# Seven block products of a feed-forward pair, woven between ordinary slots

## The chip, the cores and the metric

The kernel runs on one core of one Trainium2 chip. The metric is the device time of one execution in microseconds; the kernel before takes 2487.53 us, the median of three runs (2485.97 to 2489.61). The engines are TensorE (PE in the profile, its weight loads PEld), VectorE (DVE), ScalarE (ACT), GpSimd (POOL) and SyncE (SP), which issues nearly all DMAs from one queue, in order.

## The reference

Two transformer-like layers run on 256 positions of width 2048, in float32. The part that the change touches is the feed-forward of the second layer:

```
h2 = rmsnorm(x, g_ffn)                      # 256 x 2048
gu = h2 @ w_gu                              # 2048 x 11264: gate half and up half
x  = x + (silu(gu[..., :5632]) * gu[..., 5632:]) @ w_down
```

The output has to agree with this float32 reference.

## The kernel before

**Tiles.** Positions are two tiles of 128 (`TT`), an output chunk is 512 columns (`W`), and a weight slot is 256 rows by 512 columns (`KS` = 2 blocks of 128 rows, 512 KB). To keep float32 accuracy every weight slot is split in two: ACT rounds it (`w_hi`, L1282), DVE takes the remainder (`w_lo`, L1945), and PE makes three matmuls in the place of one (activation high by weight low, high by high, low by high). An ordinary slot is 12 matmuls: 2 row blocks, 2 position tiles, 3 parts. `raw`, `w_hi` and `w_lo` are rings of 4 buffers. So slot g can be rounded when PE is done with slot g-4 (semaphore `slot_used`), its remainder follows, and PE waits for `lo_ready`. A raw buffer is free for the next load when the remainder is taken.

**Blocks and pairs.** The feed-forward runs in three blocks (`ff_block`) of 4, 4 and 3 pairs, each followed by a down projection. A pair makes one chunk of 512 gate columns (unit 0, `acc[:, 0]`) and the same chunk of up columns (unit 1, `acc[:, 1]`), over 8 slots of weight rows for each.

**Quad products.** In all pairs but the first, ten in number, the first two weight-row slots of gate and up (a two by two arrangement of weight blocks against a two by two arrangement of activation blocks) are not multiplied as eight block products but as seven, by sums of blocks (a Strassen-Winograd scheme). A product slot is 6 matmuls. The four weight blocks of a pair land in `quad_raw` (`load_quad`, L469; block 0 and 1 are gate and up of the first rows, 2 and 3 of the second), four in-place additions on DVE (`quad_add`, L1928, semaphore `quad_sum`) form the sums between the remainders that need them, and each sum is again rounded and split. The other 12 slots of a pair are ordinary (`after_quad`, L827 to L829).

**Order in a pair.** The seven products are slots 0 to 6, in the accumulators `tp[0]`, `acc[0,0]`, `po`, `sc`, `tp[1]`, `acc[0,1]`, `acc[1,0]`; slots 7 to 12 are gate and 13 to 18 up. ACT and DVE each walk a list written out by hand: roundings or remainders of the slots, and between them the rest. For ACT that is a copy of `tp[0]` (L1324), the silu of the gate chunk (L1334), the joining of transposed planes (L917) and their rounding (L928). For DVE it is the sum that ends the previous pair's up chunk (`up_out`, L2027), the gated product (L2018), its split in two 16-bit planes (L1406), three combining additions (L2060, L2064, L2068), the gate chunk (L2078) and the remainder of the joined planes (`lo_of`, L1414).

**SP's queue.** `load_ff` loads raw slot r when raw slot r-4 has had its remainder taken. The next pair's four blocks follow the loads 4 to 7 of a pair. The previous pair's planes are transposed by two DMAs (`turn_planes`, L366) ahead of load 6. A wait holds everything behind it on the queue.

Of the kernel before, what the change touches and what calls it, by code (L numbers as in the profile page):

```python
# [67 lines left out]
def feed_forward_slots():  # L68
# [46 lines left out]
def build_program(nc, t):  # L115
    ctx = ExitStack()
    with ctx:
# [232 lines left out]
        def _(sp):  # L350
# [121 lines left out]
            for b in range(3):  # L472
                for j in range(FF_PAIRS[b]):
# [3 lines left out]
                    for i in range(2 * n):  # L477
# [3 lines left out]
                        if j and i == n:  # L481
                            turn_planes(X_FF + b * NCH + j - 1, "ff")
                        load_ff(r + i, gate_up(b, j, unit, s))
                        if j < FF_PAIRS[b] - 1 and 4 <= i < 8:
                            load_quad(p + 1, i - 4)
                _, r = FF_DOWN[b]
                n = FF_SLOTS[b]
                for i in range(NCH * n):
# [4 lines left out]
                    if b < 2 and 20 <= i < 24:  # L493
                        load_quad(4 * b + 4, i - 20)
# [13 lines left out]
        def _(pe):  # L508
# [274 lines left out]
            def quad_product(g, f, out, xh, xl, start, stop=False):  # L783

                pe.wait_ge(lo_ready, g + f + 1)
                ring = (g + f) % RING
                for k in range(KS):
                    wh, wl = w_hi[:, ring, k, :], w_lo[:, ring, k, :]
# [9 lines left out]
            def quad_slots(p, u):  # L798
# [17 lines left out]
            def after_quad(g0, unit):  # L816

                for s in range(Q0, SPU):
                    g = g0 + s - Q0
                    pe.wait_ge(lo_ready, g + 1)  # L820
                    for k in range(KS):
                        for tk in range(TT):
                            kt, out = KS * s + k, acc[:, unit, tk, :]
                            xh, xl = (part[:, kt, tk * P:(tk + 1) * P] for part in (a_hi, a_lo))
                            wh, wl = w_hi[:, g % RING, k, :], w_lo[:, g % RING, k, :]
                            first = (unit, tk, s, k) == (1, 1, Q0, 0)
                            nc.tensor.matmul(out, xh, wl, start=first, stop=False)  # L827
                            nc.tensor.matmul(out, xh, wh, start=False, stop=False)  # L828
                            mm = nc.tensor.matmul(out, xl, wh, start=False,  # L829
                                                  stop=s == SPU - 1 and k == KS - 1)  # L830
                    mm.then_inc(slot_used, 1)

            def ff_block(b):
# [3 lines left out]
                for j in range(pairs):  # L837
                    p = pair_of(b, j)
                    g, _, quad = FF_PAIR[p]
                    if quad:  # L840
                        quad_slots(p, u + 2 * j)
                        after_quad(g + QUAD, 0)
                        after_quad(g + QUAD + SPU - Q0, 1)
# [1403 lines left out]
```

## Time and profile before

| what | value |
|---|---|
| median of three runs | 2487.53 us |
| profiled execution | 2487.44 us, span 2485.6 us, granted clock 0.999 |
| PE busy | 2466.3 us (99%) |
| DVE busy | 1608.4 us (65%) |
| ACT busy | 1409.5 us (57%) |
| DMA queue of SP | 66.1% of 16 engines' time |
| chain that ended last | PE 89%, DVE 6%, DMA 2%, ACT 2% |

The span is the time from the first to the last instruction of the execution that was profiled, and 1.84 us lie around it. Matmuls overlap, so that PE counts as busy nearly always; what it loses is read from its idle time and from the distance between starts of matmuls. The pairs lie between 1806 and 2404 us of the span, with the down projections between them.

### The profile page before, as it was taken

What the parts mean: (1) busy time and instruction counts of PE and PEld (TensorE: products, weight loads), DVE (VectorE), ACT (ScalarE), POOL (GpSimd) and SP (SyncE); (2) the same over time, 40 slices, a digit from 0 to 9 for tenths busy, and PEclk for the clock granted to TensorE, in tenths of its full rate; (3) what the DMA queues carried; (4) which work ended last, traced back from release to release, by engine and by line L of the source; (5) the groups of instructions that cost most, each with busy time, mean ns of one, the idle gap of its engine ahead of it and who ended that gap; (6) DMA issues with size and microseconds to landing.
All of it is one profiled execution on the core that took longest, in us unless ns stands there. A gap on an engine that the chain in (4) does not pass through costs nothing.

```text
span 2485.6 us, 28783 instructions
## 1 busy us (share of the span) xinstructions
PE 2466.3 (99%) x10957; PEld 2038.9 (82%) x10957; DVE 1608.4 (65%) x1743; ACT 1409.5 (57%) x1716; POOL 67.0 (3%) x78
## 2 busy tenths in 40 slices
PE   9999999999999999999999999999999999999999
PEld 8888888888888888888888888888787888788887
DVE  5988576556555565666577645556587567866774
ACT  6886566455455465556666644546555445554453
POOL 0110000000000000011100000000000000000000
PEclk9999999999999999999999999999999999999999
DMA  8997668677677676577766666667757765575755
GB/s 287 262 268 205 203 191 223 208 215 226 195 210 209 192 218 196 161 222 213 218 185 206 193 196 202 203 187 221 223 167 212 232 198 185 172 222 183 237 176 169
DMA packets 348554, 515.34 MB, mean 207 GB/s; under 512 B 113840, under 2 KB 114152, under 8 KB 348168
## 3 DMA queue, kind: packets, MB, share of 16 engines
q1 hardware_dynamic: 343592, 496.63, 66.1%
q0 software_dynamic: 4688, 16.93, 3.0%
q8 instruction: 86, 1.41, 0.2%
q14 instruction: 44, 0.36, 0.0%
q10 hardware_dynamic: 144, 0.01, 0.0%
HBM read 476.52 MB, written 4.47 MB: 194 GB/s over the span
## 4 chain that ended last, share of the span: by engine, by line
PE 89%; DVE 6%; DMA 2%; ACT 2%; issue 1%; SPq 1%; POOL 0%; DVEq 0%; ACTq 0%; POOLq 0%
PE acc L531 26%; PE acc L533 26%; PE acc L532 26%; DVE w_lo L1945 3%; PE acc L829 3%; PE acc L828 3%; PE acc L827 3%; DMA raw<-w_gu_dram 1%; DVE quad_raw L1928 1%; ACT w_hi L1282 1%; DMA planesT_mix<-planes_mix 0%; ACT joined_ff L917 0%; SPq L366 0%; DVE ev L2027 0%; PE tp L567 0%
## 5 line engine op out<-in xcount | busy, mean ns | idle before, releaser
L1371 DVE TENSOR_TENSOR w_lo<-raw,w_hi 128x1024 fp32r<-128x1024 f32 x628 | 761.2, 1224 | 539.6 <-ACT w_hi L880 539.0
L880 ACT ACTIVATE w_hi<-raw 128x1024 fp32r<-128x1024 f32 x628 | 659.3, 1059 | 639.1 <-PE acc L533 628.4
L531 PE MATMUL acc<-w_lo,a_hi 128*128 128x512 f32 x1664 | 652.2, 392 | 4.0 <-DVE a_lo L1420 3.2
L533 PE MATMUL acc<-w_hi,a_lo 128*128 128x512 f32 x1664 | 648.7, 390 | 0.0
L532 PE MATMUL acc<-w_hi,a_hi 128*128 128x512 f32 x1664 | 648.5, 390 | 0.0
L531 PE MATMUL acc<-w_lo,b_hi 128*128 128x512 f32 x1104 | 430.0, 389 | 0.3 <-DVE w_lo L1371 0.3
L532 PE MATMUL acc<-w_hi,b_hi 128*128 128x512 f32 x1104 | 429.5, 389 | 0.0
L533 PE MATMUL acc<-w_hi,b_lo 128*128 128x512 f32 x1104 | 429.5, 389 | 0.0
L1945 DVE TENSOR_TENSOR w_lo<-raw,w_hi 128x1024 fp32r<-128x1024 f32 x220 | 267.3, 1223 | 184.2 <-ACT w_hi L1282 183.3
L1282 ACT ACTIVATE w_hi<-raw 128x1024 fp32r<-128x1024 f32 x220 | 232.0, 1059 | 250.4 <-PE acc L533 111.8
L531 PEld LDWEIGHTS acc<-w_lo,a_hi 128*128 128x128 f32 x1664 | 313.1, 188 | 69.4 <-DVE a_lo L1420 3.7
L533 PEld LDWEIGHTS acc<-w_hi,a_lo 128*128 128x128 f32 x1664 | 313.0, 188 | 65.9
L532 PEld LDWEIGHTS acc<-w_hi,a_hi 128*128 128x128 f32 x1664 | 313.2, 188 | 64.2
L531 PEld LDWEIGHTS acc<-w_lo,b_hi 128*128 128x128 f32 x1104 | 207.2, 188 | 43.5 <-DVE w_lo L1371 0.7
L533 PEld LDWEIGHTS acc<-w_hi,b_lo 128*128 128x128 f32 x1104 | 207.2, 188 | 43.1
L532 PEld LDWEIGHTS acc<-w_hi,b_hi 128*128 128x128 f32 x1104 | 207.2, 188 | 43.0
L827 PE MATMUL acc<-w_lo,a_hi 128*128 128x512 f32 x480 | 186.7, 389 | 0.0
L828 PE MATMUL acc<-w_hi,a_hi 128*128 128x512 f32 x480 | 186.7, 389 | 0.0
L829 PE MATMUL acc<-w_hi,a_lo 128*128 128x512 f32 x480 | 186.7, 389 | 0.0
L1282 ACT ACTIVATE w_hi<-quad_raw 128x1024 fp32r<-128x1024 f32 x70 | 72.7, 1058 | 70.1 <-DVE quad_raw L1928 34.2
L828 PEld LDWEIGHTS acc<-w_hi,a_hi 128*128 128x128 f32 x480 | 90.1, 188 | 18.7
L827 PEld LDWEIGHTS acc<-w_lo,a_hi 128*128 128x128 f32 x480 | 90.1, 188 | 18.7
(259 smaller groups left out, 1900.8 us busy)
## 6 DMA issues: line engine op xcount, KB each, us to landing
raw<-w_in_dram SPq DMA_DIRECT2D x272, 512.0 KB, 4.5
raw<-w_down_dram SPq DMA_DIRECT2D x216, 512.0 KB, 4.2
raw<-w_gu_dram SPq DMA_DIRECT2D x136, 512.0 KB, 4.6
raw<-w_up_dram SPq DMA_DIRECT2D x128, 512.0 KB, 3.8
raw<-w_out_dram SPq DMA_DIRECT2D x64, 512.0 KB, 4.2
quad_raw<-w_gu_dram SPq DMA_DIRECT2D x40, 512.0 KB, 5.8
raw<-w_branch_dram SPq DMA_DIRECT2D x32, 512.0 KB, 4.2
tap_sum<-tap_add POOLq DMA_DIRECT2D x20, 512.0 KB, 7.1
```

Of the source, the lines that this page charges most:

```text
L531: nc.tensor.matmul(out, xh, wl, start=s == 0 and k == 0, stop=False)
L532: nc.tensor.matmul(out, xh, wh, start=False, stop=False)
L533: mm = nc.tensor.matmul(out, xl, wh, start=False, stop=s == n - 1 and k == KS - 1)
L827: nc.tensor.matmul(out, xh, wl, start=first, stop=False)
L828: nc.tensor.matmul(out, xh, wh, start=False, stop=False)
L829: mm = nc.tensor.matmul(out, xl, wh, start=False, stop=s == SPU - 1 and k == KS - 1)
L880: nc.scalar.activation(w_hi[:, ring], raw[:, ring], ACT.Copy).then_inc(hi_ready, 1)
L1282: nc.scalar.activation(w_hi[:, g % RING], src, ACT.Copy).then_inc(hi_ready, 1)
L1371: nc.vector.tensor_tensor(w_lo[:, ring], raw[:, ring], w_hi[:, ring].bitcast(F32), ALU.subtract).then_inc(lo_ready, 1)
L1928: nc.vector.tensor_tensor(quad_raw[:, to // 2, to % 2], quad_raw[:, one // 2, one % 2], quad_raw[:, other // 2, other % 2], ALU.add).then_ ...
L1945: nc.vector.tensor_tensor(w_lo[:, g % RING], src, w_hi[:, g % RING].bitcast(F32), ALU.subtract).then_inc(lo_ready, 1)
```

## The change

The seven products become slots 0, 2, 4, 6, 8, 10 and 12 of the pair, and the six ordinary gate slots lie between them as slots 1, 3, 5, 7, 9 and 11. The order of the products is new (accumulators `tp[0]`, `po`, `sc`, `acc[1,0]`, `tp[1]`, `acc[0,0]`, `acc[0,1]`). The up slots stay 13 to 18. The four additions stand after the remainders of slots 0, 1, 5 and 9. The next pair's blocks are loaded in the order 1, 3, 2, 0 after the loads 6, 7, 9 and 10 of a pair (after loads 17, 20, 23 and 26 of a down projection), each with waits of its own. The transposes move ahead of load 10. On DVE and ACT the combining additions, the planes' split, the silu and the joining stand at later places, among the up slots. No matmul, rounding, remainder, addition or load is added or taken away.

The diff, cut to its core ("..." marks what is left out):

```diff
@@ feed_forward_slots
             if quad:
-                kind += [(f, None) for f in range(QUAD)]
+                for f in range(QUAD):
+                    kind += [(f, None)] + [(None, r + f)] * (f < SPU - Q0)
             n = 2 * (SPU - Q0 if quad else SPU)
-            kind += [(None, r + i) for i in range(n)]
+            kind += [(None, r + i) for i in range(n // 2 if quad else 0, n)]
@@ sync: load_quad
-                if i == 0:
-                    if quad_of(p):
-                        sp.wait_ge(lo_ready, FF_PAIR[p - 1][0] + QUAD)
-                    else:
-                        sp.wait_ge(slot_used, G_FF)
+                if quad_of(p) == 0:
+                    sp.wait_ge(slot_used, G_FF)
+                else:
+                    g, q = FF_PAIR[p - 1][0], quad_of(p) - 1
+                    sp.wait_ge(lo_ready, g + (13, 5, 11, 7)[i])
+                    sp.wait_ge(quad_sum, 4 * q + (4, 2, 4, 3)[i])
...
-                        if j and i == n:
+                        if j and i == (10 if quad else n):
                             turn_planes(X_FF + b * NCH + j - 1, "ff")
                         load_ff(r + i, gate_up(b, j, unit, s))
-                        if j < FF_PAIRS[b] - 1 and 4 <= i < 8:
-                            load_quad(p + 1, i - 4)
+                        if j < FF_PAIRS[b] - 1 and (i if quad else i - 4) in (6, 7, 9, 10):
+                            load_quad(p + 1, {6: 1, 7: 3, 9: 2, 10: 0}[i if quad else i - 4])
@@ tensor: quad_pair (before: quad_slots and two after_quad)
-                quad_product(g, 0, tp[:, 0, :], *tile_of(0, 0), True, True)
+                quad_product(g, tp[:, 0, :], tile_of(0, 0))
                 pe.wait_ge(evacuated, u - 1)
-                quad_product(g, 1, acc[:, 0, 0, :], *tile_of(1, 0), True)
-                quad_product(g, 2, po[:, :], x_hi[:, 0], x_lo[:, 0], True, True)
-                quad_product(g, 3, sc[:, :], x_hi[:, 1], x_lo[:, 1], True, True)
-                quad_product(g, 4, tp[:, 1, :], x_hi[:, 2], x_lo[:, 2], True, True)
-                quad_product(g, 5, acc[:, 0, 1, :], *tile_of(1, 1), True)
+                other_slot(g + 1, 0, 2)
+                quad_product(g + 2, po[:, :], sum_of(0))
+                other_slot(g + 3, 0, 3)
+                quad_product(g + 4, sc[:, :], sum_of(1))
+                other_slot(g + 5, 0, 4)
                 pe.wait_ge(evacuated, u)
-                quad_product(g, 6, acc[:, 1, 0, :], x_hi[:, 3], x_lo[:, 3], True)
+                quad_product(g + 6, acc[:, 1, 0, :], sum_of(3), stop=False)
+                other_slot(g + 7, 0, 5)
...
+                quad_product(g + 12, acc[:, 0, 1, :], tile_of(1, 1), start=False)
                 for s in range(Q0, SPU):
+                    other_slot(g + 13 + s - Q0, 1, s)
@@ scalar: order of a pair
-                    uses(g + 5, g + 16)
-                    if j:
-                        join(j - 1)
-                    uses(g + 16, g + 17)
-                    if j:
-                        rounded(j - 1)
-                    uses(g + 17, g + 18)
+                    uses(g + 5, g + 18)
                     ... the silu
-                    uses(g + 18, g + 19 + RING)
+                    if j:
+                        join(j - 1)
+                    uses(g + 18, g + 19)
+                    if j:
+                        rounded(j - 1)
+                    uses(g + 19, g + 19 + RING)
@@ vector: quad_sums, called after the remainder of slot g
+                if i == 0:
+                    dve.wait_ge(quad_in[1], 16 * (q + 1))
+                    dve.wait_ge(lo_ready, g + 1)
+                    quad_add(0, 1)
+                elif i == 1:
+                    dve.wait_ge(quad_in[3], 16 * (q + 1))
+                    dve.wait_ge(quad_sum, 4 * q + 1)
+                    quad_add(1, 3)
+                elif i == 5:
+                    dve.wait_ge(lo_ready, g - 2)
+                    quad_add(0, 3)
+                elif i == 9:
+                    dve.wait_ge(quad_in[2], 16 * (q + 1))
+                    dve.wait_ge(lo_ready, g)
+                    quad_add(0, 2)
@@ vector: order of a pair
-                    uses(g + 4, g + 8)
+                    uses(g + 4, g + 5)
                     if j:
                         gated_product(j - 1)
-                    uses(g + 8, g + 9)
+                    uses(g + 5, g + 13)
                     if j:
                         part_planes("ff", zz, (z_ready, z + j))
...
```

DVE where one pair ends and the next begins (the last two names of a row are what is read; `w_lo<-quad_raw` is the remainder of a product slot, `w_lo<-raw` of an ordinary one, `quad_raw<-quad_raw` an addition). Before, from slot 0 of the next pair on:

```order
L1945 TENSOR_TENSOR w_lo<-quad_raw,w_hi 128x1024
L1928 TENSOR_TENSOR quad_raw<-quad_raw 128x1024
L1945 TENSOR_TENSOR w_lo<-quad_raw,w_hi 128x1024
L1928 TENSOR_TENSOR quad_raw<-quad_raw 128x1024
L1945 TENSOR_TENSOR w_lo<-quad_raw,w_hi 128x1024
L1928 TENSOR_TENSOR quad_raw<-quad_raw 128x1024
L1945 TENSOR_TENSOR w_lo<-quad_raw,w_hi 128x1024
L2027 TENSOR_TENSOR ev<-acc,parts_ff 128x1024
L1928 TENSOR_TENSOR quad_raw<-quad_raw 128x1024
L1945 TENSOR_TENSOR w_lo<-quad_raw,w_hi 128x1024 x3
L1945 TENSOR_TENSOR w_lo<-raw,w_hi 128x1024
L2018 SCALAR_TENSOR_TENSOR zz<-ev,rs 128x512 x2
```

The same place in the changed kernel (the line numbers have moved: L1971 is the remainder, L1936 the addition, L2043 `up_out`, L2033 the gated product):

```order
L1971 TENSOR_TENSOR w_lo<-quad_raw,w_hi 128x1024
L1936 TENSOR_TENSOR quad_raw<-quad_raw 128x1024
L1971 TENSOR_TENSOR w_lo<-raw,w_hi 128x1024
L1936 TENSOR_TENSOR quad_raw<-quad_raw 128x1024
L1971 TENSOR_TENSOR w_lo<-quad_raw,w_hi 128x1024
L1971 TENSOR_TENSOR w_lo<-raw,w_hi 128x1024
L2043 TENSOR_TENSOR ev<-acc,parts_ff 128x1024
L1971 TENSOR_TENSOR w_lo<-quad_raw,w_hi 128x1024
L2033 SCALAR_TENSOR_TENSOR zz<-ev,rs 128x512 x2
L1971 TENSOR_TENSOR w_lo<-raw,w_hi 128x1024
L1936 TENSOR_TENSOR quad_raw<-quad_raw 128x1024
L1971 TENSOR_TENSOR w_lo<-quad_raw,w_hi 128x1024
```

Ahead of the remainder of slot 4 stood four remainders, four additions and `up_out`; now it is four remainders, two additions and `up_out`.

SP's queue over one pair, before:

```order
L455 DMA raw<-w_gu_dram 128x2x512 x9
L469 DMA quad_raw<-w_gu_dram 128x2x512
L455 DMA raw<-w_gu_dram 128x2x512
L469 DMA quad_raw<-w_gu_dram 128x2x512
L366 DMA_TRANSPOSE planesT_ff<-planes_ff 128x8x128 x2
L455 DMA raw<-w_gu_dram 128x2x512
L469 DMA quad_raw<-w_gu_dram 128x2x512
L455 DMA raw<-w_gu_dram 128x2x512
L469 DMA quad_raw<-w_gu_dram 128x2x512
L455 DMA raw<-w_gu_dram 128x2x512 x10
```

And in the changed kernel:

```order
L456 DMA raw<-w_gu_dram 128x2x512 x8
L471 DMA quad_raw<-w_gu_dram 128x2x512
L456 DMA raw<-w_gu_dram 128x2x512
L471 DMA quad_raw<-w_gu_dram 128x2x512
L456 DMA raw<-w_gu_dram 128x2x512 x2
L471 DMA quad_raw<-w_gu_dram 128x2x512
L367 DMA_TRANSPOSE planesT_ff<-planes_ff 128x8x128 x2
L456 DMA raw<-w_gu_dram 128x2x512
L471 DMA quad_raw<-w_gu_dram 128x2x512
L456 DMA raw<-w_gu_dram 128x2x512 x11
```

The transposes moved behind four more loads of ordinary slots, and behind three of the four block loads in the place of two; the block that the next pair reads first is now the last that is loaded.

## Rows read from the trace of the kernel before

**Rows 1.** Waits, 1806 to 2404 us, PE and PEld: total us, times, longest.

```profile
PE tp L789 <- DVE w_lo L1945: 9.7, 9, 1.7
PE sc L789 <- DVE w_lo L1945: 0.3, 1, 0.3
...
PEld tp L789 <- DVE w_lo L1945: 13.5, 9, 2.2
PEld sc L789 <- DVE w_lo L1945: 1.3, 3, 0.8
```

**Rows 2.** Timeline of PE (start us, length us): four pair starts, one stall.

```profile
1807.05 0.39 PE L789 MATMUL tp<-w_lo,a_hi 128*128 128x512 f32 x1
...
1849.21 0.39 PE L789 MATMUL tp<-w_lo,a_hi 128*128 128x512 f32 x1
...
2110.24 0.39 PE L789 MATMUL tp<-w_lo,a_hi 128*128 128x512 f32 x1
...
2115.51 0.40 PE L791 MATMUL sc<-w_hi,x_lo 128*128 128x512 f32 x1
...
2117.65 0.50 PE L789 MATMUL tp<-w_lo,x_hi 128*128 128x512 f32 x1 [1.75 <-DVE w_lo L1945]
...
2154.50 0.39 PE L789 MATMUL tp<-w_lo,a_hi 128*128 128x512 f32 x1
```

**Rows 3.** Timeline of DVE ahead of that stall.

```profile
2112.98 1.22 DVE L1945 TENSOR_TENSOR w_lo<-quad_raw,w_hi 128x1024 fp32r<-128x1024 f32 x1
2114.11 1.22 DVE L2027 TENSOR_TENSOR ev<-acc,parts_ff 128x1024 f32<-128x1024 f32 x1
2115.25 1.22 DVE L1928 TENSOR_TENSOR quad_raw<-quad_raw 128x1024 f32<-128x1024 f32 x1
2116.38 3.57 DVE L1945 TENSOR_TENSOR w_lo<-quad_raw,w_hi 128x1024 fp32r<-128x1024 f32 x3
```

**Rows 4.** Timeline of ACT: three roundings, with the idle time before them.

```profile
1807.31 1.06 ACT L1282 ACTIVATE w_hi<-quad_raw 128x1024 fp32r<-128x1024 f32 x1 [1.66 <-PE acc L533]
...
2116.50 2.01 ACT L1282 ACTIVATE w_hi<-quad_raw 128x1024 fp32r<-128x1024 f32 x2 [1.86 <-DVE quad_raw L1928]
...
2133.37 1.06 ACT L1282 ACTIVATE w_hi<-raw 128x1024 fp32r<-128x1024 f32 x1 [4.41 <-DMA raw<-w_gu_dram]
```

**Rows 5.** Groups by line, 1806 to 2404 us, DVE, then ACT: busy us, mean ns.

```profile
L1945 DVE TENSOR_TENSOR w_lo<-raw,w_hi 128x1024 fp32r<-128x1024 f32 x182 | 221.1, 1223 | 145.2 <-ACT w_hi L1282 144.5
L1928 DVE TENSOR_TENSOR quad_raw<-quad_raw 128x1024 f32<-128x1024 f32 x38 | 46.4, 1222 | 1.5
L1406 DVE COPY planes_ff<-zz 128x1024 uint16<-128x1024 uint16 x20 | 12.9, 687 | 0.1
L2018 DVE SCALAR_TENSOR_TENSOR zz<-ev,rs 128x512 f32<-128x512 f32 x18 | 12.7, 746 | 0.2
L1414 DVE TENSOR_TENSOR b_lo<-joined_ff,b_hi 128x512 fp32r<-128x512 f32 x18 | 11.6, 686 | 5.9 <-ACT b_hi L928 5.9
...
L1282 ACT ACTIVATE w_hi<-raw 128x1024 fp32r<-128x1024 f32 x183 | 193.2, 1060 | 208.3 <-DMA raw<-w_gu_dram 91.5 <-PE acc L533 78.5 <-PE acc L829 32.1
L917 ACT ACTIVATE joined_ff<-planesT_ff 128x1024 uint16<-128x1024 uint16 x20 | 25.7, 1352 | 2.2 <-DMA planesT_ff<-planes_ff 2.2
L1334 ACT ACTIVATE ev<-ev,rs 128x512 f32<-128x512 f32 x18 | 12.0, 716 | 2.9 <-DVE ev L2078 2.9
L928 ACT ACTIVATE b_hi<-joined_ff 128x512 fp32r<-128x512 f32 x20 | 11.4, 619 | 0.0
```

**Rows 6.** Timeline of SP's queue: the two transposes of that pair.

```profile
2124.49 4.89 SPq L366 DMA_TRANSPOSE planesT_ff<-planes_ff  x2
```

**Rows 7.** Windows (us, busy us and count by engine, PEclk, DMA share, GB/s).

```profile
1776.00:1784.00 8.00, 7.06 (x19) 5.60 (x20) 5.55 (x8) 5.90 (x10) 0.00 (x0) 0.57 0.33 102
2107.00:2151.00 44.00, 42.25 (x187) 34.54 (x186) 34.32 (x35) 24.25 (x26) 0.00 (x0) 1.00 0.63 200
```

**Rows 8.** Timeline of PE: the stall at the start of the first window.

```profile
1776.94 0.79 PE L531 MATMUL acc<-w_lo,a_hi 128*128 128x512 f32 x1 [3.24 <-DVE a_lo L1420]
```

More of the change, by code:

```diff
@@ L796, in tile_of, with sum_of, other_slot, quad_pair @@
                         a_lo[:, KS * half_:KS * half_ + KS, tk * P:(tk + 1) * P])
-            def quad_slots(p, u):
+            def sum_of(n):
+                return x_hi[:, n], x_lo[:, n]
+            def other_slot(g, unit, s):
+                pe.wait_ge(lo_ready, g + 1)
+                for k in range(KS):
+                    for tk in range(TT):
+                        kt, out = KS * s + k, acc[:, unit, tk, :]
+                        xh, xl = (part[:, kt, tk * P:(tk + 1) * P] for part in (a_hi, a_lo))
+                        wh, wl = w_hi[:, g % RING, k, :], w_lo[:, g % RING, k, :]
+                        first = s == Q0 and k == 0 and (unit, tk) != (1, 0)
+                        last = s == SPU - 1 and k == KS - 1 and (unit, tk) != (0, 1)
+                        nc.tensor.matmul(out, xh, wl, start=first, stop=False)
+                        nc.tensor.matmul(out, xh, wh, start=False, stop=False)
+                        mm = nc.tensor.matmul(out, xl, wh, start=False, stop=last)
+                mm.then_inc(slot_used, 1)
+            def quad_pair(p, u):
                 g, _, _ = FF_PAIR[p]
@@ L812, in quad_slots @@
-                quad_product(g, 5, acc[:, 0, 1, :], *tile_of(1, 1), True)
-                pe.wait_ge(evacuated, u)
-                quad_product(g, 6, acc[:, 1, 0, :], x_hi[:, 3], x_lo[:, 3], True)
-            def after_quad(g0, unit):
-                for s in range(Q0, SPU):
[L819 to L831, printed above, removed]
+                other_slot(g + 1, 0, 2)
@@ new lines, in quad_pair @@
+                quad_product(g + 2, po[:, :], sum_of(0))
+                other_slot(g + 3, 0, 3)
+                quad_product(g + 4, sc[:, :], sum_of(1))
+                other_slot(g + 5, 0, 4)
+                pe.wait_ge(evacuated, u)
+                quad_product(g + 6, acc[:, 1, 0, :], sum_of(3), stop=False)
+                other_slot(g + 7, 0, 5)
+                quad_product(g + 8, tp[:, 1, :], sum_of(2))
+                other_slot(g + 9, 0, 6)
+                quad_product(g + 10, acc[:, 0, 0, :], tile_of(1, 0), start=False, stop=False)
@@ L1923, in _, with quad_add, pair_at, quad_sums @@
                 part_planes("mix", h[:, :, j], (h_ready, 2 * NCH + j + 1))
-            def quad_add(q, n, to, one, other):
-                nc.vector.tensor_tensor(quad_raw[:, to // 2, to % 2], quad_raw[:, one // 2, one % 2],
+            def quad_add(to, other):
+                nc.vector.tensor_tensor(quad_raw[:, to // 2, to % 2], quad_raw[:, to // 2, to % 2],
                                         quad_raw[:, other // 2, other % 2], ALU.add
                                         ).then_inc(quad_sum, 1)
+            def pair_at(g):
+                return max(p for p in range(len(FF_PAIR)) if FF_PAIR[p][0] <= g)
+            def quad_sums(g):
+                p = pair_at(g)
+                i, q = g - FF_PAIR[p][0], quad_of(p)
+                if not FF_PAIR[p][2]:
+                    return
+                if i == 0:
[13 more added lines that the diff above has]
+                    quad_add(0, 2)
             def use(g):
                 f, r = FF_KIND[g - G_FF]
-                if f is None:
-                    src = raw[:, r % RING]
-                else:
-                    q = quad_of(max(p for p in range(len(FF_PAIR)) if FF_PAIR[p][0] <= g))
-                    i = (0, 2, 0, 1, 0, 2, 3)[f]
-                    src = quad_raw[:, i // 2, i % 2]
-                    if f == 4:
-                        dve.wait_ge(quad_sum, 4 * q + 3)
-                        quad_add(q, 4, 2, 2, 0)
+                i = None if f is None else (0, 0, 1, 3, 0, 2, 0)[f]
+                src = raw[:, r % RING] if f is None else quad_raw[:, i // 2, i % 2]
                 dve.wait_ge(hi_ready, g + 1)
@@ L2065, in ff_block @@
                                             ).then_inc(combined, 1)
-                    uses(g + 12, g + 13)
+                    uses(g + 14, g + 15)
+                    if last and j < 2:
+                        to_h(2 * j)
+                    uses(g + 15, g + 17)
+                    dve.wait_ge(rs_ok, 6)
                     dve.wait_ge(combined, 3 * q + 2)
+                    dve.wait_ge(slot_used, g + 13)
+                    nc.vector.tensor_tensor(ev[:, 0], acc[:, 0], parts_ff[:, 0::2], ALU.add
+                                            ).then_inc(evacuated, 1)
+                    uses(g + 17, g + 18)
                     nc.vector.tensor_tensor(parts_ff[:, 1::2], parts_ff[:, 1:3],
```

51 lines of the change are left out of this document (15 added, 36 removed).

## Prediction

> **What bounds the kernel now.** I began with the waits of PE in the stretch of the pairs, because PE is nearly always busy and only its idle time can be won. There the reader is to see one kind of wait [rows 1]: PE stands before the first matmul of the product that goes to `tp` or `sc`, for a remainder of DVE, 9 + 1 times and 10.0 us in all; the weight loads, which run ahead of their matmuls, show 14.8 us for the same places.
>
> Next the timeline of PE gives the length of a pair [rows 2]. The first quad pair runs from 1807.05 to 1849.21: 42.16 us, without a stall. It holds 7 x 6 + 12 x 12 = 186 matmuls, so one starts every 0.2267 us; a product slot takes 1.36 us and an ordinary one 2.72. The pair from 2110.24 to 2154.50 takes 44.26, 2.10 more. Its stall shows 1.75 of idle time; the rest is that an idle stretch begins only after 0.39 of a matmul that would have overlapped the next by 0.16, and that the first matmul after it is longer (0.50). So each of the ten waits costs some 0.3 more than its idle time, and **the pairs lose 10.0 + 10 x 0.3 = 13.0 us**, with 10.0 and 14.8 as the bounds.
>
> Why DVE is late is in its timeline and that of ACT ahead of this stall [rows 3, 4]. Four DVE operations of 1.22 us follow each other without a pause, 1.14 us from start to start: the remainder of slot 3, `up_out`, the fourth addition, the remainder of slot 4, done at 2117.60. PE resumes at 2117.65. ACT had waited 1.86 us for an addition before it could round. Seven products take PE 9.5 us; in that time DVE owes seven remainders, four additions and `up_out`, 12 x 1.14 = 13.7 us. The ring of four lets it begin early, but not early enough. Over a whole pair DVE is busy only 34.3 of 44 us [rows 7]. The burst is too dense, the engine isn't full.
>
> **The change part by part.** Work is only moved: the same 186 matmuls, 19 roundings, 19 remainders and 4 additions in a pair. The floor of a pair stays 42.16 us, so the most to be won is 13.0.
>
> *The alternation.* I work a schedule of one pair, T being the time after its first matmul. PE's slots then end at 1.36, 4.08, 5.44, 8.16, 9.52, 12.24, 13.6, 16.32, 17.68, 20.4, 21.76, 24.48, 25.84, and each 2.72 later up to 42.16. A rounding starts 0.26 after the first matmul of the slot behind the one that frees its buffer (1807.05 to 1807.31 [rows 2, 4]) and takes 1.06; a remainder, an addition or `up_out` takes 1.22 [rows 5]. I count these in full, though back to back they come 1.14 apart, so the result is on the late side. As a test, the order of before done this way gives the remainder of slot 4 at T = 7.4 where PE wants it at 5.44, a wait of 2.0; the trace has 2.1.
>
> In the new order the end of a pair (silu, joining, rounding of planes on ACT, 2 x 0.72 + 2 x 1.35 + 2 x 0.62; their remainders on DVE, 2 x 0.69 [rows 5]) puts the next pair's remainder of slot 0 at -4.5 to -3.3. From there DVE goes on without a pause: addition 1 to -2.1, slot 1 to -0.9, addition 2 to 0.4, slot 2 to 1.6, slot 3 to 2.8, `up_out` to 4.1, slot 4 to 5.3, gated product (2 x 0.75) to 6.8, slot 5 to 8.0, addition 3 to 9.2, slot 6 to 10.4, slot 7 to 11.6. PE wants these slots at 1.36 (slot 1), 4.08, 5.44, 8.16, 9.52, 12.24 and 13.6. **The smallest margin is 1.5 us, at slot 5**; then follow slot 6 with 1.8 and slot 7 with 2.0. From slot 8 on DVE again waits for ACT: slot 9 is done at 14.8 (wanted at 17.68), slot 12 at 20.2 (24.48), and after the planes' split (2 x 0.69) and the first combining addition slot 13 at 23.5 (25.84). All the 13.0 us go by this schedule. In the ten waits' place no operation is late by it: what is next latest is slot 5, with 1.5 us to spare.
>
> *The up slots.* The combining additions, the gate chunk, the silu and the joins now lie between slots 13 and 18, where PE takes 2.72 us a slot and DVE owes one remainder for it: six slots, 16.3 us, against 7.3 us of remainders and some 7 of the rest. Cost nothing; if the cover is gone, the price is in the second rival.
>
> *Loads and SP's queue.* Block loads 1, 3 and 2 follow loads 6, 7 and 9; their own waits (a remainder and an addition) are met at T = 5.3, 10.4 and 17.2, before the waits of the loads just ahead of them (8.0, 11.6, 18.9), so they hold nothing up. The two transposes wait for the planes at T = 20.9 to 21.6; behind them stand load 10 (slot 17), block 0 of the next pair and load 11 (slot 18). Before, from the first transpose at 2124.49 to the rounding that had waited for the load behind it there went 8.9 us (2133.37 [rows 4, 6]). That puts load 10 at T = 29.8. Slot 17's rounding may start as late as 36.72 - 1.06 - 1.22 - 0.2 = 34.2: 4.4 us to spare. Block 0, one load later, is needed by 39.6. Both cost nothing. An estimate on the late side; the bounds are 0 and the rivals' prices, and not below 0, since PE has nothing else to win here.
>
> *A rule to weigh.* Twelve times a pair PE now changes between a bank that a product fills and those of the gate chunk. In the trace the seven products of before already go through `tp`, `acc`, `po`, `sc` and `tp`, with a 1.75 us stall among them, and the granted clock of that stretch is 1.00, the 2.4 GHz level [rows 2, 7]. The Trainium skill says in "TensorE: Matmul & The Clock Gate", section "A second HAM failure mode: psum-queue depth-cycling", that going round the PSUM banks with small idle times between the groups can make the clock swing between its two levels. This trace speaks against it for groups of six matmuls; by the rule the sum would be that of the last rival.
>
> **The rivals.** *First, the forecast:* all waits go, 2487.4 - 13.0.
>
> *Second, part of them comes back.* The late end of a pair is a chain: load 10, rounding of slot 17, silu, join, rounding of slot 18, rounding of planes, remainder of slot 0. With load 10 at 29.8 in the place of the 28.8 at which its buffer is free, everything up to slot 7 of the next pair comes about a microsecond later, and slot 5 has 0.4 us to spare. For it speaks that ACT stood 91.5 us for loads in this stretch [rows 5]; against it the 0.08 us by which each of the dozen DVE operations is shorter than I counted. What lateness goes beyond that, PE waits in the five quad pairs that follow a pair with a join (the third and fourth pair of the first two blocks, the third of the last). With 0.7 to 1.6 us in each: 2474.5 + 3.5 to 8, or 2478 to 2482.5.
>
> *Third, nothing is won:* the order does not take the stall away, because the second sum's chain (addition, rounding, remainder, 1.22 + 1.06 + 1.22) is as long as ever. ACT's 1.86 us for an addition [rows 4] speaks for it; against it an ordinary slot of 2.72 us now lies between any two products. 2483 to 2492.
>
> *Fourth, slower, by SP's queue.* The loads of slots 17 and 18 and of block 0 stand behind both transposes, later in the pair than before. If the first of them lands more than 13.3 us after the transposes began (4.4 more than the 8.9 seen), PE stalls at slot 17 in the eight pairs that have transposes (all ten but the first of the second and third block). The balance turns at 13.0 / 8 = 1.6 us of stall, that is, at a landing 15 us after the transposes. A stall like that of 3.24 us at 1776.94 [rows 8] takes the clock down as well: the granted clock of the 8 us around it was 0.57 [rows 7], most of the time at 1.2 GHz, a loss of 8 x 0.43 = 3.4 us. With stalls of 2.5 us: 2474.4 + 20 = 2494; with 3.24 and the clock, 2474.4 + 8 x 6.6 = 2527.
>
> *Fifth, the clock by the alternation,* the rule above as a mechanism of this kernel: the 25.84 us of alternating slots at half clock would take 25.84 more in each of ten pairs, 2474 + 258 = 2732. Nothing in the rows shows it.
>
> **How the numbers follow.** The profiled execution took 2487.44, its span 2485.6 with 1.84 around it; it stands 0.1 under the median of 2487.53, so that no correction is needed. 2487.5 - 13.0 = **2474.5 us**. The bounds of the loss give 2472.7 and 2477.5. Chances: forecast 0.72 (2472.5 to 2477.5), part of it 0.14, nothing 0.07, slower by SP 0.06, clock 0.01. The range is 2472.5 to 2481, the forecast with its bounds and most of the second case; about 0.82. A measurement of this kernel can tell about 0.2%, 5 us, from no change: faster by more is the first two cases, 0.86; within it the third, 0.07; slower the last two, 0.07.
>
> **What would show it.** Right: the waits of PE before `tp` and `sc` are gone, pairs are 42.2 us apart throughout, ACT's wait for additions (1.86 us a time here) shrinks, and the clock stays at 1.00. The second case shows PE idle before slots 5 to 7 for a remainder, in pairs with a join alone; the third still before a product; the fourth before slots 17 or 18, with ACT waiting for a raw load and SP long in the transposes. I'd be wrong in the sizes if DVE's operations grew longer where DMA and PE read the same memory more evenly, which no row can exclude.

## The result, and the profile after

The changed kernel takes **2468.09 us**, the median of four runs (2467.95 to 2468.33); the kernel before, run beside it, 2486.75 (2485.95 to 2489.61). The ratio is 0.9923, with a 95% interval of 0.9907 to 0.9938. The forecast was 2474.5 with a range from 2472.5 to 2481: the sign was right, and the time lies 4.4 us below the low end. The profiled execution took 2468.15 us with a span of 2466.3, so 19.3 us less span than before (2485.6).

What PE still waits for comes all from ahead of the pairs. These are the waits of PE in the profile after, from 0 to 1806 us (total us, times, longest). From 1790 to 2400 us the view has no line of PE, and the ten waits of [rows 1] have no successor:

```profile
PE acc L578 <- POOL mean_w L2139: 1.0, 1, 1.0
PE acc L533 <- issue: 0.7, 2, 0.3
PE acc L533 <- DVE m_lo L1422: 0.6, 1, 0.6
PE acc L533 <- DVE w_lo L1379: 0.3, 1, 0.3
```

A fifth wait is missing too, which no step of the prediction counted: the 3.24 us before the matmul at 1776.94 [rows 8]. The two windows of [rows 7], after the change:

```profile
1776.00:1784.00 8.00, 8.00 (x37) 6.63 (x36) 3.41 (x5) 4.44 (x5) 1.79 (x2) 1.00 1.02 378
2107.00:2151.00 44.00, 44.00 (x195) 36.41 (x194) 37.21 (x37) 26.37 (x28) 0.00 (x0) 1.00 0.71 212
```

In the first, PE runs 37 matmuls where it ran 19, and the granted clock is 1.00 in the place of 0.57. In the second it runs 195 for 187, with no idle time, and the clock stays at 1.00. Weight loads count 36 and 20, and 194 and 186, likewise.

Within a block the pairs are now 42.16 us apart, the floor that [rows 2] gave. Two successive pair starts with the first matmul of slot 5 between them, from the timeline of PE (by the rounding of these two rows, 42.15):

```profile
2098.88 0.39 PE L791 MATMUL tp<-w_lo,a_hi 128*128 128x512 f32 x1
...
2108.40 0.39 PE L813 MATMUL acc<-w_lo,a_hi 128*128 128x512 f32 x1
...
2141.03 0.39 PE L791 MATMUL tp<-w_lo,a_hi 128*128 128x512 f32 x1
```

The operation that the prediction named as the tightest is in DVE's timeline of the same pair: the remainder of slot 3 with a pause ahead of it, then the remainder of slot 4, the gated product and the remainder of slot 5, which answer to the row of operations in [rows 3]:

```profile
2100.23 1.23 DVE L1971 TENSOR_TENSOR w_lo<-raw,w_hi 128x1024 fp32r<-128x1024 f32 x1 [0.71 <-ACT w_hi L1291]
...
2102.51 1.22 DVE L1971 TENSOR_TENSOR w_lo<-quad_raw,w_hi 128x1024 fp32r<-128x1024 f32 x1
2103.64 1.41 DVE L2033 SCALAR_TENSOR_TENSOR zz<-ev,rs 128x512 f32<-128x512 f32 x2
2104.96 1.22 DVE L1971 TENSOR_TENSOR w_lo<-raw,w_hi 128x1024 fp32r<-128x1024 f32 x1
```

The last one ends at 2106.18, T = 7.3 (T is the prediction's time after the first matmul of the pair), and PE wants it at 2108.40: a margin of 2.2 us. Two kinds of wait of ACT (total, times, longest) have shrunk. Before they were the 91.5 us for loads in [rows 5] and, for sums, from 1806 to 2404 us:

```profile
ACT w_hi L1282 <- DVE quad_raw L1928: 34.2, 22, 1.9
```

After, from 1795 to 2400 us:

```profile
ACT w_hi L1291 <- DMA raw<-w_gu_dram: 3.9, 2, 2.0
ACT w_hi L1291 <- DVE quad_raw L1936: 3.4, 2, 1.8
```

**Where the 19.3 us came from.** The first quad pair started at 1807.05 [rows 2]; it now starts 6.0 us sooner:

```profile
1801.04 0.39 PE L791 MATMUL tp<-w_lo,a_hi 128*128 128x512 f32 x1
```

From there to the end of the span it is 678.6 us before and 665.3 after, so that the stretch of the pairs gave 13.3 us, the forecast's 13.0 and 0.3 more. The 6.0 us ahead of it are won at 1776.94 and just behind. In before, PE's matmuls start 0.227 us apart up to 1773.31 and again from 1783.02 on; this is the timeline between, at its first and last steps:

```profile
1773.31 0.39 PE L533 MATMUL acc<-w_hi,a_lo 128*128 128x512 f32 x1
...
1777.53 0.63 PE L532 MATMUL acc<-w_hi,a_hi 128*128 128x512 f32 x1
...
1783.02 0.40 PE L533 MATMUL acc<-w_hi,a_lo 128*128 128x512 f32 x1
```

From 1773.31 to 1776.94 there go 3.63 us, 3.40 more than a step. The next step takes 0.59, 0.36 too much, and the 13 steps from 1777.53 to 1783.02 take 5.49 where 2.95 would do: 0.43 a step for most of them, at a granted clock of 0.50 from 1778 to 1782 us, the 1.2 GHz level. 3.40 + 0.36 + 2.54 = **6.3 us**. The changed execution reaches this place 0.3 us later (compare the starts of the transposes below), and 13.3 + 6.3 - 0.3 = 19.3.

What PE waited for there is `a_lo`, the last part of the attention output, which reaches PE by two transposes on SP's queue, ACT (`joined_mix`, `a_hi`) and DVE. SP's queue before (start us, length us):

```profile
1757.41 0.37 SPq L469 DMA_DIRECT2D quad_raw<-w_gu_dram  x1
...
1758.34 0.47 SPq L469 DMA_DIRECT2D quad_raw<-w_gu_dram  x1
...
1759.36 0.58 SPq L469 DMA_DIRECT2D quad_raw<-w_gu_dram  x1
...
1760.53 0.47 SPq L469 DMA_DIRECT2D quad_raw<-w_gu_dram  x1
1761.69 8.28 SPq L366 DMA_TRANSPOSE planesT_mix<-planes_mix  x2
```

and after:

```profile
1752.79 7.70 SPq L456 DMA_DIRECT2D raw<-w_gu_dram  x5
1761.98 2.65 SPq L367 DMA_TRANSPOSE planesT_mix<-planes_mix  x2
...
1768.69 0.47 SPq L471 DMA_DIRECT2D quad_raw<-w_gu_dram  x1
```

The first pair has no products of its own, but it loads the blocks of the second. Before, these four loads follow its raw loads 4 to 7 and stand ahead of the transposes. Now, by the table `{6: 1, 7: 3, 9: 2, 10: 0}[... i - 4]` in the diff, they follow loads 10, 11, 13 and 14 and stand behind them (the section on the change gives loads 6, 7, 9 and 10 for every pair, which holds for the quad pairs only). The transposes start at the same time, 1761.69 and 1761.98, but hold SP 8.28 us in the one and 2.65 in the other. ACT takes their result over at 1772.68 before, with 5.56 us of idle time, and at 1766.90 after, with none:

```profile
1772.68 2.54 ACT L917 ACTIVATE joined_mix<-planesT_mix 128x1024 uint16<-128x1024 uint16 x2 [5.56 <-DMA planesT_mix<-planes_mix]
```

```profile
1766.90 2.56 ACT L926 ACTIVATE joined_mix<-planesT_mix 128x1024 uint16<-128x1024 uint16 x2
```

The difference, 5.8 us, is about what four loads of 512 KB need: in the trace before, loads issued one after the other land some 1.35 us apart, 5.4 us for four.

### The profile page after: what moved, and what is told of

The parts are those of the page before. It is cut to its first block, busy times and chain, and to the rows that moved or that the text cites. A ratio compares the mean times of both kernels' runs of the same rounds, so it can differ in the third digit from the quotient of the medians.

```text
span 2466.3 us, 28839 instructions
## 1 busy us (share of the span) xinstructions
PE 2460.2 (100%) x10957; PEld 2038.0 (83%) x10957; DVE 1609.3 (65%) x1743; ACT 1412.5 (57%) x1716; POOL 67.0 (3%) x78
## 4 chain that ended last, share of the span: by engine, by line
PE 98%; DVE 1%; ACT 0%; issue 0%; DMA 0%; POOL 0%; SPq 0%; DVEq 0%; ACTq 0%; POOLq 0%
PE acc L533 26%; PE acc L535 26%; PE acc L534 26%; PE acc L814 4%; PE acc L813 4%; PE acc L815 4%; PE acc L792 1%; PE acc L791 1%; PE acc L793 1%; PE tp L792 0%; PE tp L791 0%; PE tp L793 0%; PE tp L569 0%; PE acc L578 0%; PE po L750 0%
## 5 line engine op out<-in xcount | busy, mean ns | idle before, releaser
L1971 DVE TENSOR_TENSOR w_lo<-raw,w_hi 128x1024 fp32r<-128x1024 f32 x220 | 268.5, 1224 | 168.2 <-ACT w_hi L1291 166.7
L535 PEld LDWEIGHTS acc<-w_hi,a_lo 128*128 128x128 f32 x1664 | 312.3, 188 | 65.8
L815 PEld LDWEIGHTS acc<-w_hi,a_lo 128*128 128x128 f32 x480 | 90.1, 188 | 18.7
L813 PEld LDWEIGHTS acc<-w_lo,a_hi 128*128 128x128 f32 x480 | 90.1, 188 | 18.7
L814 PEld LDWEIGHTS acc<-w_hi,a_hi 128*128 128x128 f32 x480 | 90.1, 188 | 18.7
```

What stands on the lines that cost most here:

```text
L535: mm = nc.tensor.matmul(out, xl, wh, start=False, stop=s == n - 1 and k == KS - 1)
L815: mm = nc.tensor.matmul(out, xl, wh, start=False, stop=last)
L1971: nc.vector.tensor_tensor(w_lo[:, g % RING], src, w_hi[:, g % RING].bitcast(F32), ALU.subtract).then_inc(lo_ready, 1)
```

## The experiments

Two theories stood against each other for the part that the forecast missed: the place of the first pair's block loads (theory: their traffic is ahead of the transposes), and the rest of the change (the denser or looser pairs themselves). For the part that it had, the question was whether the alternation carries it, or the smaller moves beside it.

**The first pair's loads put back, in the changed kernel.**

```diff
-    if j < FF_PAIRS[b] - 1 and (i if quad else i - 4) in (6, 7, 9, 10):
-        load_quad(p + 1, {6: 1, 7: 3, 9: 2, 10: 0}[i if quad else i - 4])
+    if quad and j < FF_PAIRS[b] - 1 and i in (6, 7, 9, 10):
+        load_quad(p + 1, {6: 1, 7: 3, 9: 2, 10: 0}[i])
+    if not quad and 4 <= i < 8:
+        load_quad(p + 1, i - 4)
```

> The changed kernel, but the first pair (the one without products) issues the next pair's four block loads after its loads 4 to 7 again, in the order 0 to 3, as before; all quad pairs stay as changed. Queue theory: the four loads stand ahead of the transposes of the last attention-output chunk on SP's queue once more; the stall of 3.2 us for a_lo at the start of the feed-forward and the slow clock after it come back, +6.3 us on 2468.1: 2474.4 us, the pairs still 42.16 us apart. Rival (the stall went because of the new order on DVE, ACT or PE): 2468 us.

Measured: 2472.86 us (2471.93 to 2474.19), ratio 0.9938 (0.9924 to 0.9952). The stall is back at its old place, here in the timeline of PE, with the transposes on SP above it:

```profile
1761.91 8.00 SPq L367 DMA_TRANSPOSE planesT_mix<-planes_mix  x2
```

```profile
1776.85 0.50 PE L535 MATMUL acc<-w_lo,a_hi 128*128 128x512 f32 x1 [2.92 <-DVE a_lo L1430]
```

```profile
1776.00:1784.00 8.00, 6.75 (x29) 5.31 (x30) 6.21 (x8) 5.72 (x11) 0.00 (x0) 1.00 0.33 98
```

The window shows why it is 1.5 us less than expected: after 2.92 us of standing still the granted clock of this execution is 1.00. Its span is 3.8 us above that of the changed kernel, about the stall with a second one of 0.40 at 1780.26 and their steps. The other runs' spans reach 2472.3, 6.0 above. The three of the five that list a clock of 0.999 over the span are the three slowest, and the other two list 1.000. So the slow clock behind the stall comes in some executions only; the length of the stall is known of the profiled one alone.

**The same loads moved, in the kernel before, and nothing else.**

```diff
-    if j < FF_PAIRS[b] - 1 and 4 <= i < 8:
-        load_quad(p + 1, i - 4)
+    if j < FF_PAIRS[b] - 1 and (4 <= i < 8 if quad else i in (10, 11, 13, 14)):
+        load_quad(p + 1, i - 4 if quad else (10, 11, 13, 14).index(i))
```

> The kernel before, but the first pair's four block loads are issued after its loads 10, 11, 13 and 14; nothing else. Queue theory: the a_lo stall and the slow clock go, 6.3 us; the ten waits of the pairs (13.0 us) stay: 2487 - 6.3 = 2481 us. Rival: 2487 us.

Measured: 2482.05 us (2481.38 to 2483.82), ratio 0.9978 (0.9968 to 0.9988), with 2487.76 for the kernel before beside it: 5.7 us gained by the place of four loads alone. `joined_mix` starts at 1767.08 and the stall for `a_lo` is gone. The pairs' waits are left, as the waits of PE from 1790 to 2400 us show:

```profile
PE tp L789 <- DVE w_lo L1945: 9.0, 9, 1.7
PE sc L789 <- DVE w_lo L1945: 0.5, 1, 0.5
PE acc L827 <- DVE w_lo L1945: 0.2, 1, 0.2
```

These are 9.7 us in 11 places; with 0.3 for each, 13.0. Its span of 2479.8 is 13.5 above that of the changed kernel. The two parts are thus separate and add up: 5.7 here, and 14.0 between this kernel's median and that of the changed one, make 19.7, where the medians of the two kernels run side by side are 18.7 apart (2486.75 and 2468.09).

**Traffic, or the wait?** Ahead of its block loads SP waits for `slot_used`, 3.5 us once in the trace before, and that wait too had moved behind the transposes. This kernel moves the loads as above but keeps the wait where it was:

```diff
+    if p == 0 and i == 4:
+        sp.wait_ge(slot_used, G_FF)
```

> As the kernel before with the first pair's block loads moved, but SP still waits after load 4 for the end of the attention-output slots, as the first block load made it do. If the wait is what delayed the transposes: 2487 us, the a_lo stall as before. If it is the traffic of the four 512 KB loads ahead of the transposes (1.35 us of landing each): transposes land some 5 us sooner, 2481 us.

Measured: 2482.52 us (2481.37 to 2483.84), ratio 0.9976 (0.9966 to 0.9987), the same as without the wait. SP's transposes:

```profile
1762.81 2.79 SPq L366 DMA_TRANSPOSE planesT_mix<-planes_mix  x2
```

They start 0.65 us later than in the kernel without the wait, and are as short. It is the four loads ahead that delay them, and not the wait.

**Half of the traffic.** Two of the four loads ahead of the transposes, `i in (4, 5, 13, 14)`, in the kernel before.

> The kernel before, but only two of the first pair's four block loads stand ahead of the transposes (after loads 4 and 5), the other two after loads 13 and 14. Traffic theory: transposes land 2.7 us sooner than in the kernel before, the a_lo stall falls from 3.2 to 0.5 to 1 us, and without the long stall the clock stays at 2.4 GHz: 2487 - 5.5 = 2481.5 us. If the clock falls after a short stall as well: 2484 to 2485 us.

Measured: 2484.26 us (2482.5 to 2487.16), ratio 0.9985 (0.9976 to 0.9994). ACT takes the transposes over at 1770.08, 2.6 us sooner than before and 3.0 later than with none ahead; SP holds the transposes for a length between the two:

```profile
1762.06 5.34 SPq L366 DMA_TRANSPOSE planesT_mix<-planes_mix  x2
```

So each 512 KB load in front costs 1.3 to 1.5 us of delay. PE's timeline shows what reaches it:

```profile
1774.37 0.50 PE L531 MATMUL acc<-w_lo,a_hi 128*128 128x512 f32 x1 [0.29 <-DVE a_lo L1420]
```

With a second wait of 0.40, for a remainder at 1777.78, that makes this span 1.1 us longer than that of the kernel with all four moved. The medians are 2.2 us apart. That is the time expected for a clock that falls after a short stall, but the clock did not fall in the profiled execution (1.00 from 1776 to 1784 us), and of the eleven runs only the slowest, 2487.16, lists 0.999 over its span; the second slowest, 2486.8, lists 1.000. What makes the other runs longer than the profiled one is not shown.

**The margin measured with needless work.** To size the margin that the schedule by hand gave to slot 5, two needless additions of 128 x 512 (into a buffer that nobody reads) were put on DVE ahead of slot 5's remainder, then six. The changed kernel with two:

```diff
...
+    p = pair_at(g)
+    if FF_PAIR[p][2] and g - FF_PAIR[p][0] == 5:
+        for n in range(2):
+            if p > 1 or n:
+                dve.wait_ge(padded, 2 * quad_of(p) + n)
+            nc.vector.tensor_tensor(pad[:, :, :], a_hi[:, 0:KS, :].bitcast(F32),
+                                    a_lo[:, 0:KS, :].bitcast(F32), ALU.add
+                                    ).then_inc(padded, 1)
```

> The changed kernel with two needless additions of 128x512 on DVE (some 0.65 us each, 1.3 us together, into a buffer that nothing reads) ahead of the remainder of slot 5 in every quad pair. The trace of the changed kernel leaves 2.2 us between the end of that remainder and its first matmul. Slack theory: nothing moves, 2468.1 us, and the distance falls to 0.9 us. Rival (the change sits at the edge, the gain is from something else than DVE's slack): some 1 us in each of eight pairs, 2476 us.

Measured: 2468.51 us (2468.44 to 2468.71), ratio 0.9919 (0.9906 to 0.9933), and no wait of PE in the pairs. DVE's timeline:

```profile
2105.43 1.41 DVE L1977 TENSOR_TENSOR pad<-a_hi,a_lo 128x512 f32<-128x512 f32 x2
2106.76 1.22 DVE L1981 TENSOR_TENSOR w_lo<-raw,w_hi 128x1024 fp32r<-128x1024 f32 x1
```

The remainder ends at 2107.98 and the matmul starts at 2108.86: 0.9 us of the 2.2 are left. With six:

> The same with six needless additions, 3.8 us a pair. Slack theory: the 2.15 us of slack are used up and the rest is PE's: 1.65 + 0.3 for the resumed start in seven pairs, 1.5 in the first, 0.7 in the two that open a block, 16.5 us in all: 2484.6 us. If DVE's list is not what bounds the pair once it is spread: 2468 to 2470 us.

Measured: 2487.59 us (2487.27 to 2489.16), ratio 1.0 (0.999 to 1.0009): as long as the kernel before. The waits of PE, and one of the ten in the timelines of DVE and PE:

```profile
PE acc L815 <- DVE w_lo L1981: 16.1, 10, 1.9
```

```profile
2116.01 4.32 DVE L1977 TENSOR_TENSOR pad<-a_hi,a_lo 128x512 f32<-128x512 f32 x6
2120.24 1.22 DVE L1981 TENSOR_TENSOR w_lo<-raw,w_hi 128x1024 fp32r<-128x1024 f32 x1
```

```profile
2121.51 0.50 PE L815 MATMUL acc<-w_lo,a_hi 128*128 128x512 f32 x1 [1.91 <-DVE w_lo L1981]
```

The six hold DVE 4.2 us; less the 2.2 of margin that makes 2.0, and 1.91 are seen, in seven pairs. Two pairs show 0.59: the first ones of the later blocks, which have no gated product to make (1.3 us less on DVE), and the very first pair shows 1.55. All ten cost 16.1 + 10 x 0.3 = 19.1 of the 19.5 us by which the medians differ, so that the price of a wait in the prediction, its idle time and 0.3, holds. The expectation was 3.0 us lower, most of it because it counted 3.8 us for the six additions, which took 4.2.

**One operation moved out of the burst.** If the burst before was too dense by little, then `up_out` moved behind slot 4's remainder, in the kernel before, should take a good part of the waits away; if only ordinary slots between the products help, the wait should go to another slot.

```diff
+    uses(g + 4, g + 5)
     if j and (b, j) != (0, 1):
         up_out(j - 1)
-    uses(g + 4, g + 8)
+    uses(g + 5, g + 8)
```

> The kernel before, with the addition that ends the previous pair's up chunk moved on DVE's list from ahead of slot 4's remainder to behind it. Density theory (DVE owes 13.7 us in the 9.5 us of the seven products, in whatever order): PE's wait before slot 4 falls by 1.1 us, but slots 5 and 6 come 1.1 us later and PE waits there instead, at most 3 us won: 2484 to 2487 us. Rival (the one addition stood in the way): 1.1 us in six pairs and 0.7 in the next ones, 2479 to 2480 us.

Measured: 2485.91 us (2483.65 to 2488.51), ratio 0.999 (0.9981 to 0.9999), 2.0 under the kernel before. PE now waits twice in a pair:

```profile
2115.76 0.50 PE L789 MATMUL tp<-w_lo,x_hi 128*128 128x512 f32 x1 [0.61 <-DVE w_lo L1945]
...
2118.03 0.50 PE L789 MATMUL acc<-w_lo,a_hi 128*128 128x512 f32 x1 [0.61 <-DVE w_lo L1945]
```

The waits come to 7.3 us in 15 places in the place of 10.0 in ten, but the stretch from the first pair's start to the end of the span (2484.9) is no shorter:

```profile
1806.32 0.39 PE L789 MATMUL tp<-w_lo,a_hi 128*128 128x512 f32 x1
```

It is 678.6 us, as in before, so that in the profiled execution the pairs lose as much in more and shorter waits (some 0.4 each beside the idle time). The 0.7 us by which its span is below that of before lie ahead of the pairs, where the stall for `a_lo` was 2.74 us; what else is in the 2.0 us is not shown. A reordering within the burst shares the lateness out; what took it away in the changed kernel is PE's time between the products.

**The transposes ahead of load 6 again, in the changed kernel.**

```diff
-    if j and i == (10 if quad else n):
+    if j and i == n:
```

> The changed kernel, with the two transposes on SP's queue ahead of load 6 of a quad pair, as before, in the place of load 10; the planes are still split late on DVE. So SP stands from load 5 on until T = 20.2, and load 6 (slot 13, wanted at T = 25.84) lands at about 26.5: remainder at 28.8, PE stalls 3.0 us in each of the eight pairs with transposes. Queue theory: 2468.1 + 8 x 3.3 = 2494.5 us, and up to 8 x 3 us more where the clock falls: 2494 to 2519 us. If the loads have that much slack: 2468 us.

Measured: 2517.94 us (2517.82 to 2519.03), ratio 1.0119 (1.0104 to 1.0135): slower than either kernel, by 49.9 us against the changed one. The waits of PE, then ACT's rounding of that slot, and SP's transposes:

```profile
PE acc L813 <- DVE w_lo L1971: 33.3, 8, 5.1
```

```profile
2102.32 1.06 ACT L1291 ACTIVATE w_hi<-raw 128x1024 fp32r<-128x1024 f32 x1 [8.63 <-DMA raw<-w_gu_dram]
```

```profile
2095.58 2.60 SPq L367 DMA_TRANSPOSE planesT_ff<-planes_ff  x2
```

The planes are now split at T = 20.2, among the up slots. Transposes that stand ahead of load 6 wait for that, and load 6, which slot 13 needs at T = 25.8, waits with them. Each of the eight pairs with transposes stalls 4.2 us on average. At the end of each stall the granted clock falls: in a window of ten us from there it is 0.83 in seven pairs and 0.66 in the one with the longest stall, of 5.1 us. The 49.9 us are 6.2 a pair. So the new place of the transposes is no detail of the change: with the planes split as late as they are now, the alternation without it loses more than it gains.

**The loads bunched, and an addition earlier.** Two parts of the change spread things out: the block loads over the pair, and the additions between remainders. Each is taken back by itself in the changed kernel: the four loads of a quad pair together behind load 10; and the third addition behind slot 2's remainder, not slot 5's.

```diff
...
+    if j < FF_PAIRS[b] - 1 and quad and i == 10:
+        for m in (1, 3, 2, 0):
+            load_quad(p + 1, m)
```

> The changed kernel, with the next pair's four block loads (1, 3, 2, 0) issued one after the other behind load 10 of a quad pair instead of behind loads 6, 7, 9 and 10. By landings 1.35 us apart, load 10 lands at T = 29, the blocks to 34.4, load 11 at 35.7 (its rounding may start as late as 36.8), load 0 of the next pair at 37.1. Slack theory (the spread of the loads carries none of the gain): 2468.1 to 2469 us. Rival (the spread of the loads carries part of it): PE waits at slot 18 or at slots 0 and 1 of the next pair, 0.5 us or more in each of seven pairs, 2472 us and up.

```diff
-    elif i == 5:
-        dve.wait_ge(lo_ready, g - 2)
+    elif i == 2:
+        dve.wait_ge(lo_ready, g + 1)
         quad_add(0, 3)
```

> The changed kernel, with the third addition on DVE right behind the remainder of slot 2 instead of slot 5, so that three of the four additions stand in the first three slots, as before. The remainders of slots 3, 4 and 5 come 0.4 us later, against 2.2 us and more of distance to their matmuls. Slack theory (the ordinary slots between the products carry the gain, not the place of an addition): 2468.1 us. Rival (the spread of the additions carries part of it): some 0.5 us a pair, 2473 us.

Measured: 2468.54 us (2467.87 to 2469.35; ratio 0.9921, 0.9908 to 0.9935) and 2468.6 us (2467.88 to 2468.82; 0.992, 0.9907 to 0.9934). Neither differs from the changed kernel, and PE waits in neither. What they spend is slack. With the loads bunched, ACT waits more, from 1795 to 2400 us:

```profile
ACT w_hi L1294 <- DMA raw<-w_gu_dram: 11.3, 7, 2.7
ACT w_hi L1294 <- DVE quad_raw L1939: 10.9, 7, 2.0
```

and the tightest remainder, that of slot 1 in the pair from 1843.1 on, ends at 1843.86 for a matmul at 1844.51, 0.65 us ahead (3.0 in the changed kernel):

```profile
1842.64 1.22 DVE L1974 TENSOR_TENSOR w_lo<-raw,w_hi 128x1024 fp32r<-128x1024 f32 x1
```

```profile
1844.51 0.39 PE L816 MATMUL acc<-w_lo,a_hi 128*128 128x512 f32 x1
```

With the addition earlier, slot 5's margin is 1.8 us. What is left to carry the time of the pairs is the alternation, with the transposes' place; the spreading of loads and sums keeps reserves that this kernel doesn't draw on. No run takes the alternation alone out of the changed kernel.

## Why the prediction was right and wrong

**The pairs: right, within 0.3 us.** The ten waits went, and the stretch of the pairs gave 13.3 us for the term of 13.0. Pairs stand 42.16 us apart throughout, as the text said. The cause was a burst on DVE and not a full engine: moving one operation within it only moved the wait, and putting 4.2 us of work ahead of slot 5 brought back ten waits of 16.1 us.

**The schedule by hand: right in its result, late by 0.2 to 1.0 us** up to slot 7, on the side that it named. Slot 5's remainder was put at T = 8.0 and came at 7.3; its margin was 1.5 and is 2.2, the smallest of the pair as forecast; slot 6 has 2.7 for 1.8, slot 9 is done at 14.8 as worked out. "From there DVE goes on without a pause" did not hold: the remainder of slot 0 is done 0.8 us sooner than worked out, and 0.71 of the lead goes at slot 3, where DVE waits for ACT. From slot 3 on the operations back to back, counted at 1.22 each and 1.14 apart, make the difference.

**Loads and SP's queue: right for the quad pairs, and here the step that failed.** For load 10 the text gave T = 29.8, the trace has 29.0, with ACT waiting 1.88 us for it. The later transposes cost nothing there. But the step worked through the loads of the quad pairs only. The diff's table has `if quad else i - 4` in it: the first pair's loads move as well, from between raw loads 4 to 8 to behind the second pair of transposes, and that was never worked out. So the step failed at one pair in eleven: it put at nothing what was worth 6.3 us in the trace, and 5.7 between medians when these four loads alone were moved.

**Wrong: "the most to be won is 13.0" and "PE has nothing else to win here".** These sentences closed the range below. The evidence against them stood in the text's own rows: a stall of 3.24 us at 1776.94 [rows 8], 30 us ahead of the first quad pair, and a clock of 0.57 behind it [rows 7]. They were used to price what a stall of SP's making would cost in the fourth rival, 6.6 us, and the same 6.3 us were there to be won. The first view was cut to 1806 to 2404 us, the stretch of the products, while the change begins with the loads at 1757. With 13.0 + 6.3 = 19.3 the sum is 2487.4 - 19.3 = 2468.1, the time measured. To the tenth that is luck: the pairs gave 0.3 more, the stretch ahead of the stall took 0.3 more, and 6.3 holds for an execution in which the clock fell behind the stall, as it does not always.

**The rivals.** The second (part comes back at slots 5 to 7) and the third (the sums' chain) did not come: the sums still take their addition, rounding and remainder, but ACT's waits for them fell from 34.2 to 3.4 us. The fourth's mechanism is real, only not at the place where the changed kernel has the transposes; moved ahead of load 6 they cost 6.2 us a pair, near the 6.6 that the text worked out for a stall with the clock. The fifth is refuted for this kernel: PE changes accumulators at every slot of the alternation, and the granted clock over the pair is 1.00. The rule of the Trainium skill ("TensorE: Matmul & The Clock Gate", section "A second HAM failure mode: psum-queue depth-cycling") speaks of small idle times between the groups that go round the banks. In this trace groups of six matmuls go round them without any. In the kernel before and in that with `up_out` moved there are such idle times (ten of up to 1.75 us, 15 of 0.2 to 0.6), and their granted clock from 1806 to 2404 us is 1.00 as well; no run here has shorter groups.

## What to carry to other kernels

When a change moves loads, list every place at which the moved issue code runs, the unit that only prepares the next one included, and look at what stands behind and in front of each load on its queue. Search for waits of the critical engine from the first moved instruction on, and not from the first one that the change is named for; a stall that is used as a price for a rival is also a candidate for a gain. A burst of work on an engine that is two thirds busy was cured here by putting other work of the critical engine between its consumers; shuffling within the burst moved the wait.

## What the runs showed of the hardware

**Transposes behind loads.** Two transposes between buffers on the core, issued on the queue of the loads, hold SP until the loads ahead have landed: 2.65 to 2.82 us with none of the four block loads ahead, 5.34 with two, 8.00 to 8.28 with four, 1.3 to 1.4 us for each 512 KB. Before, SP is through with them at 1769.97, and the last block load ahead, issued at 1760.53, takes 9.6 us to land, to 1770.1; after, it is 1764.63, and 4.6 us from 1760.12, to 1764.7.

**The clock after a stall.** It fell after some stalls and not after others of much the same length. After 3.24 us (before) it was 0.57 in the following window; after 2.92 us at the same place, with the same work behind it, 1.00. In the run with `up_out` moved it fell after 2.74 us at that place:

```profile
1777.38 0.50 PE L531 MATMUL acc<-w_lo,a_hi 128*128 128x512 f32 x1 [2.74 <-DVE a_lo L1420]
```

```profile
1776.00:1784.00 8.00, 6.62 (x22) 5.31 (x23) 5.99 (x8) 6.34 (x12) 0.00 (x0) 0.79 0.35 102
```

With six needless additions, one of seven stalls of 1.91 us brought a fall. Here it is, beside another of the seven in a window of the same length:

```profile
2074.00:2082.00 8.00, 6.48 (x21) 5.18 (x22) 7.06 (x7) 2.51 (x3) 0.00 (x0) 0.79 0.64 198
2120.00:2128.00 8.00, 6.49 (x28) 5.37 (x29) 8.00 (x8) 3.19 (x3) 0.00 (x0) 1.00 0.62 196
```

PE ran 21 matmuls in the one and 28 in the other, after equal stalls. With the transposes early, after stalls of 4.0 to 5.1 us, it fell in all eight pairs. So a stall of 2 to 3 us can cost some 1.6 us (these seven matmuls) to 2.5 us (the 13 slow steps of before) more than itself, or nothing more.

The times of single runs show the same. Of the ten runs with six needless additions, the six that list a clock of 1.000 over the span took 2487.27 to 2487.67 us, the four that list 0.999 took 2488.81 to 2489.16. The clock is not all of the spread, though: the 21 runs of before beside them go from 2485.2 to 2490.8, and the four of these that list 1.000 alone from 2485.18 to 2489.04; why is not shown. The runs of the changed kernel, without such stalls, go from 2467.95 to 2468.33.
